# A two-block sequence kernel: how many weight tiles ahead the split runs (LEAD 4 to 5)

## The reference

```python
def first_block(x, c, ...):
    sh1, sc1, g1, sh2, sc2, g2 = split(silu(c) @ ada_w + ada_b)
    h = rmsnorm(x, norm1_g) * (1 + sc1) + sh1
    x = x + g1 * token_mixer(h)      # z = h @ w_in; NSA attention (4 groups x 4 heads) and RG-LRU
                                     # merged = sig(ga)*(o_a @ proj_a) + sig(gb)*(o_b @ proj_b); @ w_out
    h = rmsnorm(x, norm2_g) * (1 + sc2) + sh2
    x = x + g2 * conv_glu_ffn(h)     # 2048 -> 2 x 6144 -> 2048
    return rmsnorm(x, final_g)

def second_block(x, ...):
    q, k, v, a_gate, u, z, g_a, g_s = split(rms_norm(x) @ w_in)
    y_a = (sliding_window_attention(norm(q), norm(k), v) * silu(a_gate)) @ w_attn_proj
    a, b = split(gelu(s5_ssm(u)) @ w_glu + b_glu)
    y_s = (a * sigmoid(b) * silu(z)) @ w_ssm_proj
    return x + (sigmoid(g_a) * y_a + sigmoid(g_s) * y_s) @ w_out
```

## Time and profile before

| | |
|---|---|
| median of 3 runs | 2693.68 us |
| profiled execution, its own time | 2692.64 us |
| its span (first to last instruction) | 2690.9 us |
| PE busy | 2597.1 us (97%) |
| DVE busy | 1877.7 us (70%) |
| ACT busy | 1107.6 us (41%) |
| POOL busy | 227.3 us (8%) |
| data moved | 568.13 MB, mean 211 GB/s |
| PE's share of the chain that ended last | 75% (DVE 12%) |

### The profile page before, as it was taken

How to read it: one execution, slowest core, us unless ns; L and a number is a source line. 1 busy time by engine, 2 the same in 40 slices (tenths; PEclk the granted TensorE clock), 3 DMA queues, 4 the chain that set the end, 5 groups by cost and what they waited for, 6 DMA issues and landing times.

```text
span 2690.9 us, 48148 instructions
## 1 busy us (share of the span) xinstructions
PE 2597.1 (97%) x20256; PEld 2505.2 (93%) x20256; DVE 1877.7 (70%) x2519; ACT 1107.6 (41%) x1381; POOL 227.3 (8%) x190
## 2 busy tenths in 40 slices
PE   7999999989999999899999999999999999999999
PEld 5789999889999999899999999999999888899999
DVE  7865667676866674679976556654487898898563
ACT  1033456455333344444443344444444444534432
POOL 0000000000000001000466610001100000000000
PEclk9988999999999999999999999999999999999999
DMA  9974466456888886478866766665555554465664
GB/s 404 424 269 151 156 204 188 142 157 212 274 268 275 278 276 211 134 254 274 278 225 212 221 211 181 183 185 180 165 181 180 157 162 132 149 189 176 195 197 134
DMA packets 243462, 568.13 MB, mean 211 GB/s; under 512 B 17424, under 2 KB 21520, under 8 KB 228784
## 3 DMA queue, kind: packets, MB, share of 16 engines
q1 hardware_dynamic: 233776, 530.33, 60.9%
q0 software_dynamic: 9472, 34.74, 3.6%
HBM read 550.85 MB, written 14.16 MB: 210 GB/s over the span
## 4 chain that ended last, share of the span: by engine, by line
PE 75%; DVE 12%; DVEq 4%; DMA 3%; ACT 3%; issue 2%; SPq 0%; ACTq 0%; POOL 0%
PE pair L1792 65%; DVE wlo L1272 4%; DMA wraw<-ada_wT_dram 3%; ACT whi L1267 2%; DVE wraw L1248 1%; PE pair L1365 1%; PE bank L499 1%; PE pair L1798 1%; DVEq L338 1%; PE pair L1785 1%; PE states_in L684 1%; PE bank L1365 1%; PE states_in L1370 1%; PE states_in L1097 0%; PE pair L1803 0%
## 5 line engine op out<-in xcount | busy, mean ns | idle before, releaser
L1272 DVE TENSOR_TENSOR wlo<-wraw,whi 128x1024 fp32r<-128x1024 f32 x777 | 977.6, 1267 | 586.0 <-ACT whi L1267 559.5
L1267 ACT ACTIVATE whi<-wraw 128x1024 fp32r<-128x1024 f32 x777 | 813.4, 1057 | 1163.9 <-PE pair L1792 669.7
L1792 PE MATMUL pair<-h_hi,whi 128*128 128x256 f32 x3936 | 1136.3, 289 | 22.2 <-DVE h_lo L426 9.2
L1792 PE MATMUL pair<-h_lo,whi 128*128 128x256 f32 x3936 | 1121.5, 285 | 0.0
L1792 PE MATMUL pair<-h_hi,wlo 128*128 128x256 f32 x3936 | 1120.8, 285 | 0.0
L1792 PEld LDWEIGHTS pair<-h_hi,whi 128*128 128x128 f32 x3936 | 763.6, 194 | 41.5 <-issue 34.9
L1792 PEld LDWEIGHTS pair<-h_lo,whi 128*128 128x128 f32 x3936 | 763.9, 194 | 0.6
L1792 PEld LDWEIGHTS pair<-h_hi,wlo 128*128 128x128 f32 x3936 | 763.1, 194 | 0.0
L1248 DVE SCALAR_TENSOR_TENSOR wraw<-wraw,cb 128x2048 f32<-128x2048 f32 x96 | 221.4, 2309 | 58.1 <-DMA wraw<-ada_wT_dram 56.8
L1792 PE MATMUL pair<-hid_hi,whi 128*128 128x256 f32 x768 | 218.5, 284 | 0.0
L1792 PE MATMUL pair<-hid_hi,wlo 128*128 128x256 f32 x768 | 217.3, 283 | 0.0
(11 more groups left out here) (443 smaller groups left out, 3296.5 us busy)
## 6 DMA issues: line engine op xcount, KB each, us to landing
wraw<-w_in_dram SPq DMA_DIRECT2D x312, 512.0 KB, 3.7
wraw<-ada_wT_dram SPq DMA_DIRECT2D x96, 1024.0 KB, 5.8
wraw<-ffn_up_dram SPq DMA_DIRECT2D x192, 512.0 KB, 3.7
wraw<-ffn_down_dram SPq DMA_DIRECT2D x96, 512.0 KB, 4.6
wraw<-w_out_dram SPq DMA_DIRECT2D x64, 512.0 KB, 4.6
wfour<-w_in_dram SPq DMA_DIRECT2D x16, 1024.0 KB, 13.5
wraw<-proj_a_dram SPq DMA_DIRECT2D x32, 512.0 KB, 5.3
wraw<-proj_b_dram SPq DMA_DIRECT2D x32, 512.0 KB, 4.9
```

The costliest lines, as they stand in the source:

```text
L1267: sc.activation(whi[:, r, 0:w], wraw[:, PLACE[z], 0:w], ACT.Copy).then_inc(hi_ready, 1)
L1272: ve.tensor_tensor(wlo[:, PLACE[z], 0:w], wraw[:, PLACE[z], 0:w], whi[:, r, 0:w].bitcast(F32), ALU.subtract).then_inc(lo_ready, 1)
L1792: ins = te.matmul(pair[:, o, :], w[:, at_w + o * P:at_w + (o + 1) * P], x, start=(k == 0 and o % 2 == 0 and t == 0), stop=(k == last and t ...
```

## The change

One constant is changed:

```diff
--- before.py
+++ after.py
@@ -22,7 +22,7 @@
 CB = 512
 RAW = 10
 HI = 6
-LEAD = 4
+LEAD = 5
 FOUR = 4
```

## The result

The changed kernel takes 2722.20 us (median of 4 runs, 2721.07 to 2725.24), the kernel before 2693.82 (4 runs, 2692.64 to 2694.63). The ratio is 1.0107, with a 95% interval of 1.009 to 1.0125. Forecast were 2704.3 us and a range up to 2716. The direction was right; the size was 28 us where 12 were forecast, and lay outside the range.

The account below looks back on a forecast made before the run. PE, busy 97% of the span, was taken as the bound, so only its waits or clock matter. Terms 3.5 + 1.6 - 2.6 + 1.2 + 2.9 + 2.9 + 2.2 = +11.7 on 2692.6 gave 2704.3 us; 8-in-10 range 2691 to 2716.

Parts of the forecast that it names:

- unit 604: Head norm, at unit 603 in the prediction: 1.6 us to spare, step moves by 2.88, so +1.2 us.
- `bz`: Opening of the S5 recurrence, unit 618: DVE's hand-over stands behind one more split, PE waits longer for this DMA, +2.9 us.
- `sg_lo`: Gate of the S5 output, unit 762: chain starts 2.88 us later, +2.9 us of wait and +2.2 of clock.
- the compression: Compression of k: one split and an ada row go before the blocks PE waits for, +3.5 us.
- rival A: Faster: splits' lead counts, all waits for low parts vanish and job steps keep their place; about 2686 us, chance 0.10.
- the 5 and the 20: Growth of PE's total waits, in us: below 5 the ring's limit account is wrong, over 20 the resets by PE are.
- Two of the signs: Signs of being right: low-part waits down to 3 us or less; high parts' idle time for PE unchanged within some 20.
- term 2: Four attention groups with the recurrence between, 262 to 650 us: later scalings and moved ada rows sum to +1.6 us.
- terms 1 and 6: Term 1: compression of k, +3.5 us. Term 6: gate of the S5 output, unit 762, +2.9 and +2.2 us for clock.
- rival C: Much slower: every hand-over inside a step loses its unit, about 2726 us; 0.14 including what lies between it and the forecast.
- term 3: End of the first recurrence: one more split ahead has the late low part ready before DVE's scan, -2.6 us.
- term 7: Flushes, sliding attention, rest of `states`, gates, FFN halves and last steps cost nothing; 1 to 3 us wherever cover is gone.

Follow-up runs that it names:

- lag_only: Kernel before with the ring of high parts cut from 6 to 5 buffers, lead still 4 and order unchanged: 2706.89 us, 1.0053.
- first_5: Kernel before with a lead of 5 up to unit 144 and 4 from there: 2702.72 us against 2694.40, 1.0035.
- fill_5: Changed kernel with 34 unused matmuls of 512 columns in PE's wait at the compression: 2714.16 us, 1.0070 against the kernel before.
- ada_back: Changed kernel (lead 5) with each ada row run one split later, behind its old step: 2711.58 us, 1.0064 against the kernel before.

## Why the prediction was wrong in size

**Right:** the mechanism and its sign. A step stands one unit later against PE where the ring sets the pace; lag_only shows it without any change of order. The terms of unit 604 (+1.2, measured 1.5 at the step), of `bz` (+2.9, 3.2) and of `sg_lo` (2.9 + 2.2, 4.3) held. So did the 4.0 us in DVE at the compression (3.5), and that rival A's waits for low parts don't vanish: they grew. PE's waits as a whole grew by 17.6 us, between the 5 and the 20 that were named. Two of the signs failed: the waits for low parts were to fall to 3 us or less, and ACT's idle time for PE to stay within some 20 us, where it grew by 168.

**Wrong, term 2** ("-4 ... and +6 ..., I take the sum of the places", +1.6): measured +9.2. The list of places was incomplete. It had the scores and scalings (L606, L632) and left out pc (L575 to L584), where an ada row moved in ahead of L562 in the second group, and `scores_used` (L596), which waits 2.8 us in the first. Waits rose by 5.1 us here, not by 1.6. The other 4.1 are clock; first_5, with the same instructions, does not have them.

**Wrong, terms 1 and 6 on the clock:** the clock was priced once, at `sg_lo`, and credited once, at 662 us. It cost 12.0 us in all, 41% of the loss. The price of a wait was also misread: of the 6.8 us at half clock at `bz` the prediction took 3.1 for the wait itself, but the clock fell at 2037.5 and the wait ended at 2038.25, so only 0.75 were, and the same sum gives 3.0 us and not 1.8. And the stretch at the gates, which no wait precedes, was in no term. At the compression alone, fill_5 bought 8 us back. This is also why rival C's 2726 came near the result, by another way than it said: it had six scalings late by a unit and three clock dips. In fact L664's waits fell (8.1 + 5.2 to 8.0 + 2.9), which the prediction had named as a sign of being wrong, and other lines took their place.

**Wrong, term 3** (-2.6): measured -0.5. The wait for that low part fell from 2.3 to 0.3, and the half clock behind it went. But the low part of the next unit, which PE had not waited for, was 1.8 us late, and those after it 1.1 and 0.5 (0.2 and 0.6 before). The wait moved by one unit, and little was gained.

**Wrong, term 7** for the stretch up to unit 593 (0): measured +3.1: +3.7 at units 374 to 377, of which some was given back later. DVE before, and then after:

```profile
1309.08 3.90 DVE L1272 TENSOR_TENSOR wlo<-wraw,whi 128x1024 fp32r<-128x1024 f32 x2
1330.10 1.90 DVE L1272 TENSOR_TENSOR wlo<-wraw,whi 128x1024 fp32r<-128x1024 f32 x1
1331.92 3.14 DVE L1248 SCALAR_TENSOR_TENSOR wraw<-wraw,cb 128x2048 f32<-128x2048 f32 x1
```

Two splits followed each other, and the ada row came behind both. Now it stands between them. PE waited 2.1 us for the low part of unit 375 and none for that of 376, and now 0.3 and 2.6. Only the second wait was followed by 3.4 us at half clock. In ada_back, with both splits together again, there is one wait of 2.4.

Open is why a given wait draws a given stretch. The runs show that it differs between executions of the same instructions. Whether it goes by the moment at which the wait falls is not shown. The Trainium skill, "TensorE: Matmul & The Clock Gate", section "What's actually happening", says that the slow phase at a kernel's start varies between runs of one kernel, by the phase of an activity window that runs freely. It does not speak of waits in mid-kernel, but these traces vary there too: 11.3 and 16.6 us at unit 144 with equal programs. In the parts of the loss, too, only the waits can be assigned. The medians of the single stretches (+3.9, +3.6, +14.0) add up to 21.5 of 28.4, without the stretch from 145 to 592, which was not run by itself.

## What to carry to other kernels

A deeper look-ahead is not free when the buffers stay the same: where the producer already runs at the limit of its ring, whatever it does after the extra step now waits for the buffer of the next one. Before counting what is pulled forward, list every hand-over on that engine for which the busiest engine waits, or will wait with one period less of slack, and do it by the semaphore, not by the lines that wait already. And price PE's waits twice, as idle time and as clock. Here 17.6 us of waits came with 12.0 us of clock. Give that second part a range and not a number, since it differed by 5.5 us between two executions of the same instructions. Filling one wait of 3.6 us with unused matmuls gained 9.3 us (4.3 to 11.3 by the interval), which shortening it could not have given by idle time alone.

## What the runs showed of the hardware

- The same wait of 3.2 us was followed by 3.4 us at half clock in one run and by 6.8 in another; one of 2.3 us by 3.4 or by none. Two executions with the same instructions to unit 144 were 5.3 us apart there.
- The clock also fell with no wait ahead of it: at 211.4 us of the trace before, after PE had been busy at full clock for 24 us and had run matmuls of 48 columns for the last 5.8 us, it was 0.50 for 13.7 us. In other executions of the same matmuls this stretch took 17.1 and 20.5 us.
- 15 unused matmuls in a wait of 3.6 us raised the granted clock over the next 32 us from 0.73 to 1.00, and the whole kernel gained 9.3 us.
- At the compression, the 64 matmuls of 60 columns took 7.4 us at full clock after a wait of 0.2 us, and 13.9 us after a wait of 3.6.
